# Second block's front in another order with one bank more, and two weight splits moved behind a feed-forward's last gate chain

## The reference, cut to what matters

```python
def conv_glu_ffn(h, w_up, conv_w, conv_b, w_down):      # feed-forward of layers 0 and 1
    a, u = jnp.split(h @ w_up, 2, axis=-1)
    a = depthwise_causal_conv(a, conv_w) + conv_b
    return (jax.nn.silu(a) * u) @ w_down
...
# second block; W = 256
proj = u @ w_in
a_x, a_gate, p_x, c_q, c_f, c_i, c_g, s_b, s_c, s_x, gate_logits = split(proj)
y_a = rg_lru_branch(a_x, a_gate, ...)     # conv, two small block products, sqrt, scan
y_b = pool_branch(p_x, ...)               # four windowed means, one small block product, scale
y_c = hgrn2_branch(c_q, c_f, c_i, c_g, ...)
y_d = s_b * causal_depthwise_conv(s_c * s_x, w)
merged = sum_k sigmoid(gate_logits[k]) * (ys[k] @ w_branch[k])
h = h + rms_norm(merged @ w_out, ...)
```

## Time and the profile before

| what | us |
|---|---|
| median of 3 runs (lowest to highest) | 1115.45 (1115.03 to 1117.42) |
| the profiled execution's own time | 1119.47 |
| its span | 1118.2 |
| PE busy | 1059.9 (95%) |
| DVE busy | 764.4 (68%) |
| ACT busy | 540.8 (48%) |
| POOL busy | 275.0 (25%) |

### The profile page before, as it was taken

One profiled execution on the slowest core, in us unless ns is written; L12 is line 12 of the kernel. 1 busy time (PEld: TensorE's weight loads), 2 busy tenths in 40 slices (PEclk: granted clock), 3 DMA queues, 4 the chain that ended last, 5 costly groups with the idle time before them and its releaser, 6 DMA issues.

```text
span 1118.2 us, 15782 instructions
## 1 busy us (share of the span) xinstructions
PE 1059.9 (95%) x6184; PEld 894.1 (80%) x6186; DVE 764.4 (68%) x1251; ACT 540.8 (48%) x797; POOL 275.0 (25%) x382
## 2 busy tenths in 40 slices
PE   8988999999999987999999999789998989999997
PEld 6756788888887755788888887789998977888886
DVE  6985558788777985568787777866562337766665
ACT  5454565555555454565555556534333444443432
POOL 1351520000000352510000002146878990000000
PEclk9998999999999998999999999999999999999999
DMA  9431345655554342255555553522434454555541
GB/s 360 143 140 63 108 139 179 210 172 205 188 188 149 128 149 69 82 194 186 190 192 190 183 191 111 188 95 85 161 132 134 165 196 195 202 181 193 184 151 38
DMA packets 26713, 179.22 MB, mean 160 GB/s; under 512 B 2960, under 2 KB 2960, under 8 KB 6160
## 3 DMA queue, kind: packets, MB, share of 16 engines
q1 hardware_dynamic: 26640, 178.22, 45.7%
HBM read 177.16 MB, written 1.05 MB: 159 GB/s over the span
## 4 chain that ended last, share of the span: by engine, by line
PE 82%; DVE 10%; ACT 3%; POOL 2%; issue 1%; DMA 1%; SPq 0%; DVEq 0%; ACTq 0%
PE pb L596 18%; PE pb L597 9%; PE pb L622 6%; PE pb L624 6%; PE pb L623 6%; PE pb L534 5%; PE pb L535 4%; PE pb L537 4%; PE pb L559 3%; PE pb L560 3%; PE pb L561 3%; PE pb L601 3%; POOL wlo L2377 2%; PE pb L848 1%; PE pb L600 1%
## 5 line engine op out<-in xcount | busy, mean ns | idle before, releaser
L1562 DVE TENSOR_TENSOR wlo<-raw,whi 128x2048 fp32r<-128x2048 f32 x118 | 270.1, 2292 | 108.8 <-ACT whi L1147 108.8
L2377 POOL TENSOR_TENSOR wlo<-raw,whi 128x256 fp32r<-128x256 f32 x332 | 248.8, 787 | 379.3 <-ACT whi L1147 374.5
L1147 ACT ACTIVATE whi<-raw 128x2048 fp32r<-128x2048 f32 (+1 forms) x165 | 305.0, 1852 | 54.4 <-PE pb L624 21.9
L596 PE MATMUL pb<-hb,whi 128*128 128x512 f32 x840 | 302.0, 398 | 0.9 <-DVE hb L1584 0.9
L597 PE MATMUL pb<-hb,wlo 128*128 128x256 f32 x840 | 235.8, 281 | 0.0
L596 PEld LDWEIGHTS pb<-hb,whi 128*128 128x128 f32 x840 | 158.0, 188 | 35.3 <-issue 1.1
L597 PEld LDWEIGHTS pb<-hb,wlo 128*128 128x128 f32 x840 | 158.7, 189 | 5.1
L559 PE MATMUL pb<-hb,whi 128*128 128x256 f32 x376 | 110.9, 295 | 11.6 <-DVE XN L2212 5.6
L622 PE MATMUL pb<-whi,gh 128*128 128x512 f32 x288 | 114.0, 396 | 0.0
L624 PE MATMUL pb<-whi,gl 128*128 128x512 f32 x288 | 113.9, 396 | 0.0
L623 PE MATMUL pb<-wlo,gh 128*128 128x512 f32 x288 | 113.9, 395 | 0.0
(11 more groups left out here) (365 smaller groups left out, 1600.1 us busy)
## 6 DMA issues: line engine op xcount, KB each, us to landing
raw<-wst SPq DMA_DIRECT2D x160, 1024.0 KB, 4.9
raw<-wst SPq DMA_DIRECT2D x8, 512.0 KB, 3.7
gb<-gains SPq DMA_DIRECT2D x3, 512.0 KB, 5.9
X<-x SPq DMA_DIRECT2D x4, 256.0 KB, 6.7
out<-X SPq DMA_DIRECT2D x4, 256.0 KB, 2.0
PQ<-prm SPq DMA_DIRECT2D x1, 909.0 KB, 4.5
prmt<-prm SPq DMA_DIRECT2D x1, 547.0 KB, 6.0
raw<-wst SPq DMA_DIRECT2D x2, 256.0 KB, 7.3
```

Of the source, the lines that this page charges most:

```text
L596: e.matmul(both, wh[:, k, s], hb2[:, k, :, :].rearrange("p i q -> p (i q)"), start=k == 0, stop=False)
L1147: e.activation(whi[:, split_slot(m), 0:w], raw[:, m % RAW, 0:w], ACT.Copy).then_inc(*hi(m))
L1562: e.tensor_tensor(wlo[:, split_slot(m), 0:w], raw[:, m % RAW, 0:w], whi[:, split_slot(m), 0:w].bitcast(F32), ALU.subtract).then_inc(*lo_v(m))
L2377: g = e.tensor_tensor(wlo[:, split_slot(m), s], raw[:, m % RAW, s], whi[:, split_slot(m), s].bitcast(F32), ALU.subtract)
```

## The change

Three things are changed.

1. In a feed-forward of layers 0 and 1 the split `ahead(l, "down", 9, 0)` (the first tile of the next layer or block) no longer stands in front of the tanh of step 10 on ACT, and its low part no longer in front of line 1917 on DVE. Both now stand behind the last gate chain.
2. The second block's front: in 2 goes to bank 2, in 7 to bank 3, in 8 to bank 0 and in 9 to bank 1. On ACT and DVE the splits and the steps stand in another order: one split between two steps where there were two; pooling's sums come ahead of log a; the lru's root and scan go behind the short convolution.
3. Pooling's product goes from in front of the gates to behind the gate qq = 2 on PE; ACT's copy "pool out" and `keep_y(1, s4)` go behind the gate qq = 3.

```diff
@@ PE
-                proj(2, 0, act["pool in"])
+                proj(2, 2, act["pool in"])
...
-                proj(7, 1, dve["conv out"])
-                proj(8, 2, act["conv in"])
-                proj(9, 3, dve["conv prod"])
-                pw = par2("pw").rearrange("p (f c) -> p f c", f=2)
-                q.wait_ge(*dve["pool diff"])
-                bank_free(6)
-                for f in range(2):
-                    mm = e.matmul(PB[6][...], pw[:, f, :], s2[:, f, :], start=True, stop=True)
-                mm.then_inc(*mm_small("pool"))
-                free[6] = act["pool out"]
+                proj(7, 3, dve["conv out"])
+                proj(8, 0, act["conv in"])
+                proj(9, 1, dve["conv prod"])
+
+                def pool_mixed():
...
                             gate(n, qq)
+                            if n == 0 and qq == 2:
+                                pool_mixed()
@@ ACT, feed-forward
-                    if j:
+                    if 0 < j < 10:
                         ahead(l, "down", j - 1, 0)
                     q.wait_ge(*ff_conv[l, j])
                     e.activation(th, cc, ACT.Tanh, scale=0.5)
...
+                ahead(l, "down", 9, 0)      # behind the loop
@@ ACT, second block (order of the queue after)
 ahead(in 0); xc; ahead(in 1); gelu in; ahead(in 2); gelu tanh; pool in (bank 2); ahead(in 7);
 wa, wx; a; tanh a; ahead(in 8); conv in (bank 0); ahead(in 9); conv; lru root; keep_y(0)
...
-                            if n == 0 and qq == 0:
-                                q.wait_ge(*act["pool out"])
+                            if n == 0 and qq == 3:
+                                q.wait_ge(*mm_small["pool"])
+                                q.wait_ge(*dve["pool diff"])
+                                for f in range(2):
+                                    a = e.activation(s4[:, f, :], PB[6][...], ACT.Copy, scale=psc[:, f:f + 1])
+                                a.then_inc(*act("pool out"))
+                                q.wait_ge(*q.prev)
                                 keep_y(1, s4)
```

More of the change, by code:

```diff
@@ L1453, in second_block @@
                 a.then_inc(*act("xc"))
+                ahead(2, "in", 1, 0)
                 q.wait_ge(*used[tile_at[2, "in", 1, 0]])
@@ L1456, in second_block @@
                 e.activation(th[:, :, :], halves(1), ACT.Square).then_inc(*act("gelu in"))
+                ahead(2, "in", 2, 0)
                 q.wait_ge(*dve["gelu in"])
                 e.activation(th[:, :, :], th[:, :, :], ACT.Tanh, scale=float(np.sqrt(2.0 / np.pi))).then_inc(*act("gelu"))
-                ahead(2, "in", 2, 0)
+                q.wait_ge(*used[tile_at[2, "in", 2, 0]])
+                e.activation(xp, halves(2), ACT.Copy).then_inc(*act("pool in"))
+                ahead(2, "in", 7, 0)
                 for i, (dst, name) in enumerate(((T_r, "wa"), (T_i, "wx"))):
@@ L1471, in second_block @@
                 e.activation(T_r, T_r, ACT.Tanh).then_inc(*act("tanh a"))
-                q.wait_ge(*used[tile_at[2, "in", 2, 0]])
-                e.activation(xp, halves(0), ACT.Copy).then_inc(*act("pool in"))
                 ahead(2, "in", 8, 0)
-                q.wait_ge(*dve["lru square"])
-                e.activation(xc, xc, ACT.Sqrt, scale=-1.0).then_inc(*act("lru root"))
+                q.wait_ge(*used[tile_at[2, "in", 8, 0]])
+                e.activation(pr, halves(0), ACT.Copy).then_inc(*act("conv in"))
                 ahead(2, "in", 9, 0)
[L1478 to L1485, removed]
                 scw = par2("scw")
@@ L1490, in second_block @@
                 a.then_inc(*act("conv"))
+                q.wait_ge(*dve["lru square"])
+                e.activation(xc, xc, ACT.Sqrt, scale=-1.0).then_inc(*act("lru root"))
                 q.wait_ge(*dve["conv out"])
                 keep_y(0, cv)
+                psc = par2("psc")
                 going = True
@@ L2255, in second_block @@
                 more(s16[64:128, :], s8[64:128, :], 8, False)
+                ahead(2, "in", 7, 0)
+                q.wait_ge(*act["wx"])
+                for f in range(2):
+                    v = e.tensor_scalar(T_r[:, f, :], T_r[:, f, :], 1.0, lam6[4][:, f:f + 1], ALU.add, ALU.mult)
+                v.then_inc(*dve("log a"))
                 rc = par2("rcnt").rearrange("p (f q) -> p f q", f=2)
@@ L2263, in second_block @@
                 e.tensor_tensor(s2, s2, xp, ALU.subtract).then_inc(*dve("pool diff"))
-                ahead(2, "in", 9, 0)
+                q.wait_ge(*act["tanh a"])
+                e.scalar_tensor_tensor(T_i, T_i, 1.0, xc, ALU.add, ALU.mult).then_inc(*dve())
+                q.wait_ge(*q.prev)
+                e.tensor_tensor(xc, aa, aa, ALU.mult).then_inc(*dve())
+                q.wait_ge(*q.prev)
+                e.scalar_tensor_tensor(xc, xc, 1.0, T_r, ALU.add, ALU.mult).then_inc(*dve("lru square"))
+                ahead(2, "in", 8, 0)
                 scw = par2("scw")
@@ L2267, in second_block @@
                 q.wait_ge(*used[tile_at[2, "in", 9, 0]])
-                e.tensor_tensor(pr, pr, halves(3), ALU.mult).then_inc(*dve("conv prod"))
+                e.tensor_tensor(pr, pr, halves(1), ALU.mult).then_inc(*dve("conv prod"))
+                ahead(2, "in", 9, 0)
                 q.wait_ge(*act["conv"])
@@ L2276, in second_block @@
                 q.wait_ge(*q.prev)
-                e.tensor_tensor(cv, cv, halves(1), ALU.mult).then_inc(*dve("conv out"))
+                e.tensor_tensor(cv, cv, halves(3), ALU.mult).then_inc(*dve("conv out"))
+                q.wait_ge(*act["lru root"])
+                e.scalar_tensor_tensor(T_i, T_i, 0.5, xc, ALU.mult, ALU.mult).then_inc(*dve())
                 keep_y(0, cv)
+                q.wait_ge(*q.prev)
+                for f in range(2):
+                    v = e.tensor_tensor_scan(T_r[:, f, :], aa[:, f, :], T_i[:, f, :], 0.0, ALU.mult, ALU.add)
+                v.then_inc(*dve("lru"))
                 going = True
```

33 lines of the change are left out of this document (10 added, 23 removed).

## The result

| what | before | after |
|---|---|---|
| median, us (lowest to highest, runs) | 1116.41 (1115.03 to 1117.42, 4) | 1098.26 (1096.98 to 1101.06, 4) |
| ratio, 95% interval | | 0.9847 (0.9819 to 0.9874) |
| profiled execution, its span | 1119.47, 1118.2 | 1097.97, 1096.6 |

What follows compares the result with a forecast made beforehand. PE, busy 95%, bounds the kernel, so only its idle or slow time can be gained. Feed-forward ends 7.9 plus front 9.5 make 17.4 us: profiled 1119.47 to 1102.1, less 4.0 to the median, 1098.0; range 1092 to 1107.

Steps and rivals of the forecast that it cites:

- Part 1, layer 0's end: Layer 0's feed-forward end: PE's 2.47 us idle before "down" 10 and the slow clock behind it go, 4.0 us gained.
- Part 1, layer 1's end: Layer 1's feed-forward end: the same gain, with four more DVE products of the norm shifting along, 3.9 us.
- Part 2, in 2's wait: Second block's front: in 2 no longer waits for lru conv, only for its low part, 0.4 us late.
- Waits of the levels: Front's gates: products(1) waits 0.4 us for level 1; products(2) is held 0.6 by pooling's product needing bank 6.
- Part 3, the fourth products' wait: Products(3) needs bank 6, free only after ACT's pool out behind gate 3's tanh: PE stands 1.7 us.
- The chain: From gate 3's end through ACT, DVE and POOL to the second branch's first gate: 12.3 us, against 8.7 before.
- Slow clock behind it: After the 3.3 us idle before the second branch's first gate, the clock falls and costs 2.3 us.
- no slow clock: Rival: the 3.3 us idle costs nothing more and POOL is never late, 1095 us; chance 0.12.
- POOL's pace: Rival: POOL at 0.94 us a piece sets the front's pace at all gates, 5.7 less gain, 1103.7; chance 0.17.
- Half at the feed-forwards: Rival: moved low part holds DVE's additions and the clock falls anyway, 4.3 not 7.9, 1101.6 us; chance 0.10.
- Front given back: Rival: the front's waits move to later tiles, all given back at 796.64, 1107.5 us; chance 0.06.
- Lockstep: Rival: PE waits for DVE's levels behind each gate, 3.4 us a round, seven rounds, about 1122 us; chance 0.05.

Runs made afterwards that it cites:

- pool_first: Kernel after with pooling's product back in front of gate 0, pool out behind "conv" and `keep_y` behind the third gate: 1092.77 us, ratio 0.9799.
- keep_late: Kernel after with `keep_y(1, s4)` moved behind the exp and the level differences on ACT and DVE: 1096.11 us, ratio 0.9814.
- order_only: Kernel after with the old banks for in 2, 7, 8 and 9, the new queue order kept: 1100.54 us, ratio 0.9857.
- front_only: Kernel after with the feed-forward change of layers 0 and 1 undone, the new front kept: 1103.58 us, ratio 0.9884.
- after_again: Kernel after, unchanged, timed and profiled again on another chip's runs as yardstick: 1096.03 us, ratio 0.9830.
- bank_only: Kernel before with only the new banks for in 2, 7, 8 and 9, every queue in its old order: 1108.87 us, ratio 0.9939.
- pool_first_dve: As pool_first, with the low part of the second branch's first gate tile made by DVE, not POOL: 1091.57 us, ratio 0.9785.
- memset_late: As pool_first_dve, with POOL's three memsets of the scan's buffers waiting for DVE's sums, not log f: 1091.47 us, ratio 0.9786.
- p1_only: Kernel before with only the split moved behind the last gate chain in layers 0 and 1: 1109.67 us, ratio 0.9935.
- best_again: pool_first_dve unchanged, run again on one chip with memset_late: 1092.16 us, ratio 0.9790.

## Why the prediction was right, step by step

The total was right within 0.3 us, and part of that is luck. The gain forecast was 17.4; the timed runs gave 17.1 with 3 us of interval either way, and 19.0 the second time. In the profiled execution it was 21.6, so that the 1102.1 forecast for that one was 4.1 too high. Terms that were off cancelled: the slow clock was taken too large, 1.3 was given back in layer 1, and 3.6 came behind the front.

- **Part 1, layer 0's end, 4.0 forecast:** 4.2 in the profile. PE finds `gl` ready and runs "down" 10 at clock 1.00. The turning of X isn't late at all (0.2 had been allowed).
- **Part 1, layer 1's end, 3.9:** 4.2 at the turning (669.84 against 679.02, less the 4.94 ahead of it), of which 0.7 is given back up to the first "in" tile, in part in a wait for DVE's `hb` (0.24 at 674.81): 3.6. In the timed runs both ends give 7.3 against 7.9.
- **Part 2, in 2's wait 0.4:** 1.32 in one profile, 0.43 and 0.41 in two others. It was 1.3 in the three profiles where the keys' product beside the memsets took 2.21, and 0.4 where it took 1.3. It was not among my terms.
- **Waits of the levels, 0.4 before products(1) and 0.6 for bank 6:** 0.76, and none. Pooling's product stands between the gates without a wait, as forecast. But the reason given, that the gates cover it and that without the cover 4.4 and 2.3 would be back, was wrong: in pool_first it stands ahead of the gates and doesn't wait, because the order of part 2 already makes its input early.
- **Part 3, the fourth products' wait 1.7:** 1.51. **The chain 12.3:** 12.18. **The idle 3.3:** 3.13. These were worked out from rows of before alone, pool_first took the 1.51 away, and keep_late took 1.8 out of the chain and left the 1.51.
- **Slow clock behind it, 2.3:** this term was mis-sized. It was 1.5 in the profiles of after and order_only and nothing in front_only and after_again, behind an idle of 3.12 to 3.15 in all four. That is why the front alone measured 11.9 to 12.9 where the step had 9.5; the rival "no slow clock" (1095) describes after_again's 1096.03 better than the forecast does.
- **What no step had:** 2.0 us ahead before the change could reach PE, 1.3 given back in layer 1 and 3.6 behind the front. In layer 1 the profile of after has slow clock in 405 to 430 (0.73 on average), from 409 on, where before falls only at 428. The early fall stood in seven of the ten profiles with part 1 and in none of the three without it (before, front_only, bank_only); order_only, pool_first_dve and memset_late have part 1 and not the fall, so part 1 alone doesn't decide it, and its cause stays open. Of the 3.6, the wait of 1.87 stood in before and p1_only, whose front is the old one, and in none of the eleven profiles with a changed front (in all of them DVE's subtraction there took 5.25 to 5.28). The slow clock behind the idle of 2.0 stood in before, p1_only and best_again. Why a changed front changes which of DVE and POOL is held up, 100 us later, is open.

**The rivals.** POOL's pace: POOL took 0.79 us a piece at the first gates (12.67 for 16), less than the 0.94 of before, and no gate of the first branch waited for it, so the forecast loss of 5.7 did not come. DVE paid instead: beside POOL the two differences of level 1 took 0.84 and 0.96, where those of level 4, with POOL idle, took 0.42 each; this lies ahead of the 0.76 before products(1). The rule of the Trainium skill (GPSIMD Engine Reference, Key points) names DVE instructions in a 2-port performance mode or with two SBUF inputs. The runs agree where POOL subtracts, though not to one size: DVE's 128x2048 subtraction with two SBUF inputs took 2.46 in before, beside a POOL piece of 2.79, and 5.26 in after. Beside POOL's memsets it kept 2.29 (memset_late), while a product with one source was stretched, from 0.43 to 2.21; whether that product ran in such a mode no row shows. Half at the feed-forwards: ruled out by p1_only's interval. Front given back: only 3.13 and 1.51 came back of what was taken. Lockstep: one wait for a level, 0.76, then none.

## What to carry to other kernels

When work is moved behind an engine's last gate, write out the whole chain from that gate to the next tile's first matmul, queue by queue: here rows of the old trace gave it to 0.1 us, and it also named the two instructions (pool out and `keep_y`) whose move won another 0.3%. When an order makes an input early, measure the cover for its lateness alone: here the kernel is faster without the cover. Price the idle times from such chains, but carry a slow clock behind an idle of 2 to 3 us as a range (here nothing to 1.6 us), not as a term. Two edits that each remove the same wait (here another bank, and another order) don't add up: measure or work out each alone.

## What was not expected of the hardware

- The same program and the same idle gave two clocks: 3.13 us of idle were followed by 0.77 in one execution and 1.00 in another; an idle of 2.00 was followed by 0.75 before, one of 1.99 at the same gate by 1.00 after. The idle of 2.47 before "down" 10 was followed by a slow clock each of the six times it stood in a profile (5.8 us for 18 matmuls).
- Where DVE and POOL both subtract, either can be the one held up, and by far more than its own length: a POOL piece of 0.70 took 2.79 (before), a DVE subtraction of 2.28 took 5.26 (after) while seven POOL pieces ran on at 0.70. POOL's 24 pieces around it took 20.33 in before and p1_only and 18.30 in bank_only, order_only and front_only. What decides which of them waits is not shown.
- A DVE product of 128x512 with one source started each time some 0.07 us before POOL's second memset of three, and took 0.43, 1.31 or 2.21 us. With 0.43 the second memset took 1.24 rather than 0.95; with 1.31 the third did, and the product ended 0.29 behind the second's end (696.07 + 1.31 = 697.38; the second ended at 697.09); with 2.21 none was longer, and the product ended 0.28 behind the third (698.77 against 698.49). It reads as if the product waited for a gap between memsets and then held the next one for 0.29; the rows fit this, and nothing here tested it.
